# Differential attention: GpSimd instead of VectorE subtracts the rounded from the full queries of rounds 2 to 7

## The reference, cut to what matters

```python
def diff_attention(q, k, v, lam):          # 4 heads, two maps of 64 columns each, ALiBi, causal
    for i in range(S // Q_BLOCK):          # 8 blocks of 128 queries
        s = jnp.einsum('bqhjd,bkhjd->bhjqk', qb, kb).astype(jnp.float32) * scale
        s = s - slopes[None, :, None, None, None] * dist
        s = jnp.where(dist >= 0, s, -jnp.inf)
        p = jax.nn.softmax(s, axis=-1)
        a = p[:, :, 0] - lam * p[:, :, 1]
        outs.append(jnp.einsum('bhqk,bkhe->bqhe', a.astype(vb.dtype), vb))
```

## Time and profile before

| | before |
| --- | --- |
| median of 3 runs | 3276.43 us (3276.31 to 3279.67) |
| the profiled execution, its own time | 3277.4 us |
| its span | 3275.6 us |
| granted TensorE clock | 0.997 |
| PE / PEld / DVE / ACT / POOL busy | 99% / 81% / 65% / 35% / 46% |
| differential attention, first and second layer | from about 1317 to 1424 us and 2439 to 2546 us |

### The profile page before, as it was taken

How to read it: one execution, slowest core, us unless ns; L and a number is a source line. 1 busy time by engine, 2 the same in 40 slices (tenths; PEclk the granted TensorE clock), 3 DMA queues, 4 the chain that set the end, 5 groups by cost and what they waited for, 6 DMA issues and landing times.

```text
span 3275.6 us, 42321 instructions
## 1 busy us (share of the span) xinstructions
PE 3229.3 (99%) x16337; PEld 2642.4 (81%) x16337; DVE 2142.0 (65%) x2915; ACT 1145.8 (35%) x2094; POOL 1503.3 (46%) x975
## 2 busy tenths in 40 slices
PE   8999999999999999999999999999999999999998
PEld 7888878888878888787888888888877878888886
DVE  6786755787657135877666675631469776767656
ACT  2230451230452001765333344510028543333444
POOL 4535324435324434236556544534342566656443
PEclk9999999999999999999999999999999999999999
DMA  4112103112101111003322363311110222233642
GB/s 162 39 53 68 61 27 90 46 35 85 64 27 40 57 39 53 32 15 125 113 106 100 110 234 141 126 45 52 39 65 8 100 86 98 97 120 123 234 153 91
DMA packets 98875, 275.06 MB, mean 84 GB/s; under 512 B 22912, under 2 KB 23296, under 8 KB 89216
## 3 DMA queue, kind: packets, MB, share of 16 engines
q1 hardware_dynamic: 76448, 241.20, 20.5%
q10 hardware_dynamic: 22240, 31.27, 2.9%
HBM read 214.24 MB, written 58.98 MB: 83 GB/s over the span
## 4 chain that ended last, share of the span: by engine, by line
PE 85%; DVE 7%; issue 3%; POOL 2%; ACT 1%; DMA 1%; DVEq 0%; POOLq 0%; SPq 0%; ACTq 0%
PE ps L1543 34%; PE ps L955 27%; PE ps L1008 6%; PE ps L1030 5%; PE ps L984 2%; PE ps L1182 2%; PE ps L1221 2%; PE ps L1132 2%; PE ps L1106 1%; DVE sl_r L2917 1%; DVE st L2327 1%; PE ps L1197 1%; POOL w_lo L797 1%; POOL w_hi L794 1%; DVE in_lo L2197 0%
## 5 line engine op out<-in xcount | busy, mean ns | idle before, releaser
L1543 PE MATMUL ps<-sl_r,sl_r 128*128 128x512 f32 x5544 | 1265.6, 390 | 6.3 <-DVE sl_r L2853 3.4
L1543 PEld LDWEIGHTS ps<-sl_r,sl_r 128*128 128x128 f32 x5544 | 1040.7, 188 | 229.9 <-DVE sl_r L2853 6.0
L794 POOL TENSOR_TENSOR w_hi<-w_raw,ones_r 128x512 fp32r<-128x512 f32 x268 | 334.2, 1247 | 982.7 <-PE ps L955 578.4
L955 PE MATMUL ps<-in_hi,w_hi 128*128 128x512 f32 x1504 | 471.5, 395 | 10.9 <-DVE in_lo L2197 9.8
L955 PE MATMUL ps<-in_lo,w_hi 128*128 128x512 f32 x1504 | 466.0, 391 | 0.0
L955 PE MATMUL ps<-in_hi,w_lo 128*128 128x512 f32 x1504 | 465.1, 390 | 0.0
L797 POOL TENSOR_TENSOR w_lo<-w_raw,w_hi 128x512 fp32r<-128x512 f32 x268 | 403.1, 1504 | 21.0
L852 POOL TENSOR_TENSOR sl_r<-sl,sl_r 128x1024 fp32r<-128x1024 f32 x92 | 249.2, 2720 | 312.3 <-ACT sl_r L1948 299.5
L955 PEld LDWEIGHTS ps<-in_hi,w_hi 128*128 128x128 f32 x1504 | 279.5, 189 | 70.3 <-issue 11.0
L955 PEld LDWEIGHTS ps<-in_hi,w_lo 128*128 128x128 f32 x1504 | 282.8, 188 | 60.2 <-issue 0.3
L955 PEld LDWEIGHTS ps<-in_lo,w_hi 128*128 128x128 f32 x1504 | 282.9, 188 | 59.6
(11 more groups left out here) (264 smaller groups left out, 4888.5 us busy)
## 6 DMA issues: line engine op xcount, KB each, us to landing
w_raw<-w_in SPq DMA_DIRECT2D x136, 512.0 KB, 3.2
raw_pair<-w_ffn SPq DMA_DIRECT2D x68, 1024.0 KB, 5.0
sl<-op_kept SPq DMA_DIRECT2D x70, 512.0 KB, 5.1
op_kept<-sl SPq DMA_DIRECT2D x44, 512.0 KB, 3.0
op_kept<-st SPq DMA_DIRECT2D x22, 512.0 KB, 2.7
x_put_away<-xt SPq DMA_DIRECT2D x16, 512.0 KB, 8.2
xt<-x_put_away SPq DMA_DIRECT2D x16, 512.0 KB, 9.9
op_kept<-st SPq DMA_DIRECT2D x22, 256.0 KB, 2.0
```

The lines of the kernel that those rows point to most:

```text
L794: pool.tensor_tensor(w_hi[:, j, cols], w_raw[:, j, cols], ones[:, 0:1].broadcast_to([P, HALF]), ALU.mult).then_inc(pool_own, 1)
L955: last = pe.matmul(ps[:, (2 * j if bank is None else bank) + h, :], w[:, w_slot, (w_k + k) * P:(w_k + k + 1) * P], part[:, k0 + k, h * HAL ...
L1543: last = pe.matmul(ps[:, to[name], :], ring(sl_r, p, wp[w])[:, k * P:(k + 1) * P], part, start=(name in ("P1", "P5") and k == 0 and wp is ...
```

## The change

The subtraction of rounds 2 to 7 leaves VectorE's step list and becomes `query_rest` on GpSimd, the same form (128 partitions, 4 x 128 columns). GpSimd does round 2 before the root of round 0, rounds 3 and 4 after the roots of rounds 0 and 1, and round n+3 after the root of round n for n = 2 to 4. Rounds 0 and 1 stay on VectorE; so round 2's on GpSimd first waits until VectorE has counted up `dif_lo` six times.

```diff
+            def query_rest(l, n):
+
+                if n == 2:
+                    pool.wait_ge(dif_lo.handle, dif_lo.at(1, l, 6))
+                pool.wait_ge(dif_hi.handle, dif_hi.at(1, l, 4 + n + 1))
+                cols = slice(n * P, (n + 1) * P)
+                pool.tensor_tensor(st_r[:, 4:8, cols], st[:, 4:8, cols], dif_q_hi[:, n % 2].bitcast(F32), ALU.subtract
+                                   ).then_inc(dif_lo.handle, 1)
+
             def split(stack, l, pair, free=None, heads=False):
...
                 for j in range(2):
                     if heads and j:
+                        query_rest(l, 2)
                         head_root(l, 0)
+                        query_rest(l, 3)
                         head_root(l, 1)
+                        query_rest(l, 4)
 
                     pool.wait_ge(raw_in[j].handle, block0 * 8 + 16)
...
                 if heads:
                     for n in range(2, NB - 1):
                         head_root(l, n)
+                        if n + 3 < NB:
+                            query_rest(l, n + 3)
...
                     if u < len(units) and kind == "dif":
                         map_scores(u, 1)
-                    if u % 4 == 2 and 2 <= u // 4 + 1 < NB and kind == "dif":
-                        dif_query_lo(l, u // 4 + 1)
```

## The result

The changed kernel takes 3285.96 us (median of 10 runs, 3283.63 to 3289.34) where the kernel before takes 3277.04 us (10 runs, 3274.61 to 3279.67): a ratio of 1.0028 with an interval of 1.0019 to 1.0037. It is slower by 8.9 us. The forecast for the median was 3282.4 us, 6.0 us slower, read as "no difference".

What follows compares the result with a forecast made beforehand. TensorE, busy 99% of the span, was taken as the bound. Rounds 3, 4, 6 and 7 add 1.0 + 0.5 + 0.8 + 0.7 = 3.0 us per layer, 6.0 in both: 3282.4 us from a median of 3276.43, range 3275.3 to 3286.2.

Steps and rivals of the forecast that it cites:

- the mechanism: A GpSimd instruction reading SBUF blocks VectorE's next instruction with two SBUF inputs, about 1.0 us beside a subtraction.
- round 3: Behind root 0, VectorE's line 2407 is held; TensorE, already waiting at 1338.23, idles 1.0 us more per layer.
- round 4: Behind root 1, TensorE's product comes 1.0 us later, part is regained by 1356.05; taken as 0.5 us per layer.
- round 5: VectorE's line 2392 is 0.4 us late, but TensorE doesn't idle for VectorE before 1381.86; 0 us.
- round 6: Line 2392 and the maps are 0.8 us late, TensorE's gap at 1381.86 grows; 0.8 us per layer, nothing given back.
- round 7: Line 2407 and the scores come 1.1 us late, TensorE takes back 0.41 at 1402.81; 0.7 us per layer.
- line 2421 stays at 0.69: Sign against the forecast: VectorE's line 2421 in rounds 0 and 1 keeps 0.69 us instead of taking about 1.7.
- B: Rival: meetings happen but VectorE's idle spots absorb most; only round 3 is left, 1.0 us per layer, 3278.4 us; chance 0.26.
- C: Rival: GpSimd's instruction falls between VectorE's two-input ones, leaving the removal's 2.0 to 2.8 us gain, 3274.0 us; chance 0.15.
- the granted clock is 1.00 in both stretches: Read from the profile before: TensorE's clock is full in both stretches; the sum has no term for it.
- no transfer is issued or passed: Said of the added GpSimd subtractions: they issue and pass no transfer; no time was counted for one.
- A: Rival: same lock, delay never given back; rounds 2, 3, 4, 6, 7 sum to 4.2 us per layer, 3284.8 us; chance 0.25.

Runs made afterwards that it cites:

- all_but_3: The changed kernel, but VectorE keeps round 3's subtraction and GpSimd does those of rounds 2, 4, 5, 6 and 7: 3283.43 us (1.0018).
- gap_two: The kernel before, GpSimd untouched, with two spare VectorE subtractions in the heads of round 0 alone: 3282.97 us (1.0017).
- same_as_after: The changed kernel timed once more, unchanged, against the kernel before: 3285.52 us (1.0024).
- timed_by_mix: The changed kernel, but GpSimd's subtraction also waits for a VectorE mix, and a late weight split starts one unit later: 3275.15 us (0.9994 to before).

## Why the prediction was right, and where it failed

**Right: the mechanism and its sum.** 6.0 us were forecast for the two stretches, and 6.06 were measured in the profile. Term by term, by how much later TensorE is behind each gap than before: round 3 1.1 us (forecast 1.0; alone 1.07), round 4 1.0 and then 0.4 given back, 0.7 in all (0.5), round 5 nothing (0; alone 0.03 on average), round 6 0.8 (0.8), round 7 1.0 and then 0.5 given back, 0.5 (0.7). That the sum is right to 0.1 us is in part luck: the terms of rounds 4 and 7 are off by 0.2 each and cancel. The sum against the profiled execution was 3283.4 us, and that execution took 3284.4.

**Right: the marks.** GpSimd's line 782 has a mean of 1.29 us in the first stretch (1.3 to 1.5 forecast). The gap of round 3 is 1.43 (1.2 to 1.5), TensorE's idle time in a stretch 5.6 us (5.5). Wrong is the instruction that pays: line 2421 was to take 1.7 us in the first two meetings, but GpSimd starts 0.09 us ahead of VectorE's line 2406, and this one is held for the same time. The forecast had named "line 2421 stays at 0.69" as a sign that B or C holds. It stays there in these two meetings, and neither holds: that sign watched one of two instructions that can be held. The groups show both:

```profile
L2421 DVE TENSOR_TENSOR rfac<-st,small 128x512 f32<-128x512 f32 x6 | 5.1, 855 | 0.2
...
L2406 DVE TENSOR_TENSOR small<-small 128x4 f32<-128x4 f32 x6 | 4.2, 698 | 1.2 <-POOL small L774 1.2
```

**Wrong: "no difference", and the time by 3.6 us.** The forecast put 3282.4 us just inside 0.2% and read "no difference"; 1.0028 (1.0019 to 1.0037) is slower. Two steps failed.

The first is the resolution: "what a measurement of this kernel can tell from no change is about 0.2%, 6.6 us". The interval here reaches 0.0009 to either side, 3.0 us, so a slowdown of the forecast's own 6.0 us would have been told from none; all_but_3 at 1.0018 (1.0009 to 1.0028) was. The forecast, read by its sum, said slower.

The second is the step from the gaps to the time, "the granted clock is 1.00 in both stretches": true of before, and taken for the changed kernel without a word. A gap was priced at its own length, and 6.0 us stood where 8.9 were measured (the other 0.6 us of the 3.6 are before's median, 3276.43 over 3 runs and 3277.04 over 10). In fact a gap of 1.4 us is followed in some executions by a clock of 1.2 GHz, which costs 1.2 to 1.3 us more in the changed kernel's stretches. In 3 of its 8 stretches this fell in, so an execution pays (1.23 + 1.23 + 1.30) / 4 = 0.9 us on average. gap_two shows that a gap, there of 1.8 us, is enough for it without GpSimd. The timed runs agree in size: the eleven of same_as_after have a mean granted clock of 0.9955 and before's 33 on the same chip 0.9960, and among those 33 a clock lower by 0.001 goes with 1.3 us more, which makes 0.8 us.

The later transfer behind the second stretch, 0.6 us, is a third term, at nothing in the forecast ("no transfer is issued or passed"). That leaves the sum at 6.1 + 0.9 + 0.6 = 7.6 us, where the two timings gave 8.9 and 8.1. The rest of 0.5 to 1.3 us is open. Part of it can be the count, since eight stretches are few: with the half clock in 6 of 8 its term would be 1.9 us in place of 0.9. The four executions of the changed kernel spend 3060.9, 3059.9, 3062.7 and 3061.8 us outside the stretches, the mean 3061.3, against 3060.8 as the mean of two of before; this difference of 0.5 us is the late transfer's size and smaller than those between executions of one kernel. For all_but_3, 6.2 us over before by median, the stretches give 4.2 us and the transfer 0.5. Its timed runs have a clock of 0.9957 where before's have 0.9964, which by the like reckoning (1.4 us for 0.001) is another 0.9, though its three profiles don't show where; 0.6 us stays open.

**The rivals.** A said that the delay is never given back: wrong, since 0.4 us are given back at the scores of round 4 and 0.5 at those of round 7, though its time of 3284.8 lies nearest to the measured one, for another reason. B (swallowed) falls with the gaps of rounds 4, 6 and 7. C (GpSimd falls between the two-input instructions) is what timed_by_mix does when made to; the change itself ties GpSimd to the root that VectorE waits for, as the forecast argued against C.

## What to carry to other kernels

Before GpSimd takes a large SBUF-reading instruction over from VectorE, look at what releases it and what VectorE does right then: started by the event for which VectorE waits too, it holds VectorE's next two-input instruction, however tiny, for nearly all of its length; started as VectorE turns to data in a bank, it costs next to nothing. Where a busy TensorE gets a new gap of 1.4 us or more (those up to 1.21 us brought none here), add a term for the clock behind it, by what the granted clock shows behind such gaps, and don't expect its length alone. And before a small sum is read as "no difference", ask how narrow the interval of the runs will be.

## What the runs showed of the hardware that was not expected

- TensorE's clock fell to half (1.2 GHz) behind a single gap of 1.4 to 1.8 us in a stretch in which TensorE was otherwise hardly idle (5.6 us of 107 in all, the gap included), not every time at the same gap (5 of 12 at 1.4 us, 2 of 2 at 1.8), at a cost of 1.2 to 1.5 us.
- A VectorE instruction on four numbers a partition took 1.22 us in place of 0.16, and one on a single number 1.33 in place of 0.22, beside one GpSimd subtraction of 1.28 us. They were let go 0.13 and 0.20 us ahead of GpSimd's recorded end.
- GpSimd's memsets of 0.51 us in the same places cost VectorE nothing (0.16 and 0.69 us as before).
- With rests made on GpSimd, ScalarE waits 1.0 us longer for one transfer some 175 us behind the second stretch, and TensorE is about 0.6 us later there, in all eleven such profiles and in none of the seven others; the reason is open.
